# Gate and up of two chunks at a time with seven block products instead of eight, in three feed-forward stages

## The reference, cut to what matters

```python
h = (jax.nn.silu(u @ gate) * (u @ up)) @ down      # gate, up: 1024 x 2816, down: 2816 x 1024
```

## Time and profile before

| | us |
|---|---|
| median of 3 runs | 1923.45 (1923.35 to 1923.48) |
| the profiled execution | 1923.51 |
| its span | 1921.70 |
| busy in it: TensorE / weight loads | 1906.2 / 1682.8 |
| VectorE / ScalarE / GpSimd | 714.2 / 1083.8 / 1546.7 |

### The profile page before, as it was taken

One profiled execution on the slowest core, in us unless ns is written; L12 is line 12 of the kernel. 1 busy time (PEld: TensorE's weight loads), 2 busy tenths in 40 slices (PEclk: granted clock), 3 DMA queues, 4 the chain that ended last, 5 costly groups with the idle time before them and its releaser, 6 DMA issues.

```text
span 1921.7 us, 28382 instructions
## 1 busy us (share of the span) xinstructions
PE 1906.2 (99%) x11290; PEld 1682.8 (88%) x11290; DVE 714.2 (37%) x1440; ACT 1083.8 (56%) x1450; POOL 1546.7 (80%) x1228
## 2 busy tenths in 40 slices
PE   9999999999999999999999999999999999999998
PEld 7888999988888888889999888888999998888887
DVE  3222867521311222138574231113677632122112
ACT  7554674456644575456734665446666667545443
POOL 7998786666899799979776759997767787888995
PEclk9999999999999999999999999999999999999999
DMA  8554543143655565555323536555444444455552
GB/s 323 197 188 173 211 143 130 53 175 124 222 195 194 182 231 197 189 183 196 134 88 110 192 116 215 182 195 208 152 158 142 150 158 153 176 178 205 197 182 104
DMA packets 48803, 331.50 MB, mean 173 GB/s; under 512 B 5536, under 2 KB 6432, under 8 KB 10656
## 3 DMA queue, kind: packets, MB, share of 16 engines
q1 hardware_dynamic: 44208, 314.61, 45.6%
q10 hardware_dynamic: 4464, 15.09, 2.3%
HBM read 328.63 MB, written 1.05 MB: 172 GB/s over the span
## 4 chain that ended last, share of the span: by engine, by line
PE 96%; ACT 1%; DVE 1%; DMA 0%; issue 0%; ACTq 0%; DVEq 0%; SPq 0%
PE bank L2001 20%; PE bank L1967 16%; PE bank L1968 16%; PE bank L1969 16%; PE bank L2007 11%; PE bank L2115 2%; PE bank L2139 2%; PE bank L2117 1%; PE bank L2457 1%; PE bank L2473 1%; PE bank L2080 1%; ACT arena L431 1%; PE bank L2719 1%; PE bank L2579 1%; PE bank L2558 1%; PE bank L2129 0%
## 5 line engine op out<-in xcount | busy, mean ns | idle before, releaser
L400 POOL TENSOR_TENSOR wlo<-raw,whi 128x512 fp32r<-128x512 f32 x1180 | 1496.1, 1306 | 317.6 <-ACT whi L431 317.2
L431 ACT ACTIVATE whi<-raw 128x2048 fp32r<-128x2048 f32 (+1 forms) x298 | 566.8, 1904 | 189.2 <-PE bank L1969 161.8
L431 ACT ACTIVATE arena<-bank 128x512 f32<-128x512 f32 (+4 forms) x389 | 210.6, 551 | 441.4 <-PE bank L2007 265.3
L2001 PE MATMUL bank<-uT,whi 128*128 128x512 f32 x1632 | 388.9, 390 | 0.0
L2001 PEld LDWEIGHTS bank<-uT,whi 128*128 128x128 f32 x1632 | 302.8, 188 | 60.6
L1967 PE MATMUL bank<-uT,whi 128*128 128x256 f32 x768 | 222.5, 290 | 0.0
L1968 PE MATMUL bank<-uT,whi 128*128 128x256 f32 x768 | 217.1, 283 | 0.0
L1969 PE MATMUL bank<-uT,wlo 128*128 128x256 f32 x768 | 217.1, 283 | 0.0
L2007 PEld LDWEIGHTS bank<-uT,wlo 128*128 128x128 f32 x1632 | 209.2, 191 | 7.9
L2007 PE MATMUL bank<-uT,wlo 128*128 128x256 f32 x1632 | 211.7, 283 | 0.0
L1967 PE MATMUL bank<-whi,uT 128*128 128x512 f32 (+1 forms) x416 | 160.8, 387 | 0.0
(11 more groups left out here) (322 smaller groups left out, 2704.9 us busy)
## 6 DMA issues: line engine op xcount, KB each, us to landing
raw<-in_w SPq DMA_DIRECT2D x295, 1024.0 KB, 4.8
rows<-in_rows ACTq DMA_DIRECT2D x22, 512.0 KB, 5.0
raw<-in_w SPq DMA_DIRECT2D x4, 512.0 KB, 6.8
arena<-in_mem ACTq DMA_DIRECT2D x2, 1024.0 KB, 8.8
x<-in_x SPq DMA_DIRECT2D x2, 512.0 KB, 5.5
arena<-in_amask ACTq DMA_DIRECT2D x1, 576.0 KB, 6.3
out<-x SPq DMA_DIRECT2D x1, 512.0 KB, 2.7
out<-arena SPq DMA_DIRECT2D x1, 512.0 KB, 2.7
```

Source lines behind the costliest of these rows:

```text
L400: r = pool.tensor_tensor(wlo[n % LAND][:, k], raw[n % LAND][:, k], whi[n % RING][:, k].bitcast(F32), ALU.subtract)
L431: return act.activation(o, i, f, **k)
L2001: pe.matmul(both, w[0][:, c], parts[:, :, k, :], start=start and k == 0, stop=False)
```

## The change

For blocks i = 0 to 3 of each of the three stages, chunks c = 2 + 2i and c + 1 are taken together. With tokens in two halves, the 1024 inputs in two halves and the two chunks as column halves (each 256 gate and 256 up columns), the eight block products of 128 tokens x 512 inputs x 512 columns become seven: three on weights as they come (w11, w22, w21) and four on sums of weights (1: w12 - w11; 2: w22 - sum 1; 3: w22 - w12; 4: w21 - sum 2), with four sums of quarters of u. VectorE makes the sums in float32 and their low parts; ScalarE splits the four sums besides the units, so its list of splits (`ORDER`) has nine entries for two chunks; unit w12 is neither split by ScalarE nor by GpSimd. w21 lands in a slot of its own in the arena. All chunks are now computed by token, with four transposes for each. The partial sums of bank 4 are copied out by ScalarE between products and added by VectorE. The down units change their order (1, then 3 and 2, 5 and 4, 7 and 6, and at the end 9, 8, 10). The other two feed-forward stages are as before; semaphores `gate_sum`, `h_sum`, `up_low` and so on are merged. Waits on `unit_done` count places in the new order.

```diff
+BLOCKS = 4
+BLOCK_FFNS = [L * LAYER_UNITS + 69 for L in range(DEPTH)] + [DEPTH * LAYER_UNITS + 60]
+EXTRA = LAND
...
+def block_units(f, i):
+    n = BLOCK_FFNS[f] + 5 + (6 * i - 1 if i else 0)
+    return {"w11": n, "w12": n + 1, "w22": n + 2, "next_rows": n + 3, "w21": n + 4, "rows": n + 5 if i else None}
+def tensor_order():
+    order, n = [], 0
+    while n < N_UNITS:
+        if n - 5 not in BLOCK_FFNS:
+            order.append(n)
+            n += 1
+            continue
+        f = BLOCK_FFNS.index(n - 5)
+        for i in range(BLOCKS):
+            u = block_units(f, i)
+            order += [u["w11"], u["next_rows"], (f, i, 2), u["w22"], (f, i, 1), u["w21"], (f, i, 3)]
+            order += [u["rows"], (f, i, 4)] if i else [(f, i, 4)]
+        n = u["rows"] + 1
+    return order
+ORDER = tensor_order()
...
+PLACE = {o: q for q, o in enumerate(ORDER)}
+FULL = {block_units(f, i)["w12"]: (f, i) for f in range(len(BLOCK_FFNS)) for i in range(BLOCKS)}
+APART = [block_units(f, i)["w21"] for f in range(len(BLOCK_FFNS)) for i in range(BLOCKS)]
...
-                if n >= LAND:
-                    sp.wait_ge(sems["unit_done"], n - LAND + 1)
-                sp.dma_start(raw[n % LAND][:], a["w"][n]).then_inc(sems[f"raw_landed{n % LAND}"], 16)
+                before = [m for m in range(n) if SLOT[m] == SLOT[n]]
+                if before and before[-1] in FULL:
+                    sp.wait_ge(sems["sums_ready"], sums(*FULL[before[-1]], 3))
+                elif before:
+                    sp.wait_ge(sems["unit_done"], PLACE[before[-1]] + 1)
+                sp.dma_start(raw[SLOT[n]][:], a["w"][n]).then_inc(sems[f"raw_landed{SLOT[n]}"], 16)
...
+                pool.wait_ge(sems["w_hi"], q + 1)
+                if n in sums_read:
+                    pool.wait_ge(sems["sums_ready"], sums_read[n])
...
+                    n = ORDER[q]
+                    if n in SLOT:
+                        full = raw[SLOT[n]]
+                        act.wait_ge(sems[f"raw_landed{SLOT[n]}"], landed(n))
+                    else:
+                        full = wsum[n[2] - 1]
+                        act.wait_ge(sems["sums_ready"], sums(*n))
+                    if q >= RING:
+                        act.wait_ge(sems["unit_done"], q - RING + 1)
+                    fn(whi[q % RING][:], full[:], AF.Copy).then_inc(sems["w_hi"], 1)
...
+            def ffn_blocks(u0):
+                f = BLOCK_FFNS.index(u0)
+                chunk_by_token(u0, 0, lambda: activation_sums(f))
+                chunk_by_rows(u0, 1, False, True)
+                for i in range(BLOCKS):
+                    c = 2 + 2 * i
+                    u = block_units(f, i)
+                    if i:
+                        token_gate(c - 2, 1, 6)
+                    split()
+                    copy_part(0, 4, u["w11"])
+                    if i:
+                        token_hi(c - 2, 6)
+                    split()
+                    split()
+                    copy_part(1, 4, (f, i, 2))
+                    split()
+                    if i:
+                        split()
+                    copy_part(2, 4, (f, i, 1))
+                    token_gate(c + 1, 0, 7)
+                    split()
+                    split()
+                    token_gate(c, 0, 5)
+                    split()
+                    token_gate(c + 1, 1, 4)
+                    split()
+                    token_hi(c + 1, 7)
...
+            def copy_part(s, b, operand):
+                act.wait_ge(sems["unit_done"], PLACE[operand] + 1)
+                fn(part_copy[s], bank[b][:, :], AF.Copy).then_inc(sems["part_out"], 1)
...
+            def weight_sum(f, i, j, parts=(0, 1, 2, 3)):
+                u = block_units(f, i)
+                first, second = {1: ("w12", "w11"), 2: ("w22", 1), 3: ("w22", "w12"), 4: ("w21", 2)}[j]
+                for name in (first, second):
+                    if parts[0] == 0 and name in u:
+                        dve.wait_ge(sems[f"raw_landed{SLOT[u[name]]}"], landed(u[name]))
+                full = raw[SLOT[u[first]]]
+                less = raw[SLOT[u[second]]] if second in u else wsum[second - 1]
+                for n in parts:
+                    k = slice(n * quarter, (n + 1) * quarter)
+                    r = tt(wsum[j - 1][:, k], full[:, k], less[:, k], ALU.subtract)
+                if parts[-1] == 3:
+                    r.then_inc(sems["sums_ready"], 1)
+            def weight_sum_lo(f, i, j):
+                q = PLACE[(f, i, j)]
+                dve.wait_ge(sems["w_hi"], q + 1)
+                for n in range(4):
+                    k = slice(n * quarter, (n + 1) * quarter)
+                    r = tt(wsum_lo[j - 1][:, k], wsum[j - 1][:, k], whi[q % RING][:, k].bitcast(F32), ALU.subtract)
+                r.then_inc(sems["sum_lo"], 1)
+            def activation_sums():
+                dve.drain()
+                tt(u_full, uT[0].bitcast(F32), uT[1].bitcast(F32), ALU.add)
+                dve.drain()
+                u11, u12 = u_full[:, 0:4, 0:P], u_full[:, 4:8, 0:P]
+                u21, u22 = u_full[:, 0:4, P:SEQ], u_full[:, 4:8, P:SEQ]
+                tt(u_sums[:, 0], u21, u22, ALU.add)
+                tt(u_sums[:, 2], u11, u21, ALU.subtract)
+                dve.drain()
+                tt(u_sums[:, 1], u_sums[:, 0], u11, ALU.subtract)
+                dve.drain()
+                tt(u_sums[:, 3], u12, u_sums[:, 1], ALU.subtract).then_inc(sems["sums_ready"], 1)
+            def activation_sums_lo():
+                dve.wait_ge(sems["hi_part"], p.count("hi_part"))
+                tt(S_parts[1], u_sums.rearrange("p a b c -> p (a b c)"), S_parts[0].bitcast(F32), ALU.subtract)
...
+            def ffn_blocks(f):
+                activation_sums()
+                chunk_by_token(0)
+                weight_sum(f, 0, 1)
+                activation_sums_lo()
+                chunk_by_rows(1, False, None)
+                weight_sum(f, 0, 2)
+                weight_sum(f, 0, 3)
+                dve.drain()
+                weight_sum(f, 0, 4)
+                for i in range(BLOCKS):
+                    c = 2 + 2 * i
+                    more = i + 1 < BLOCKS
+                    weight_sum_lo(f, i, 2)
+                    if i:
+                        token_lo(c - 2, 6)
+                    weight_sum_lo(f, i, 1)
+                    weight_sum_lo(f, i, 3)
+                    dve.wait_ge(sems["part_out"], 3 * (f * BLOCKS + i) + 3)
+                    tt(bank[7][:, :], bank[7][:, :], part_copy[2], ALU.add).then_inc(sems["sum_out"], 1)
+                    if more:
+                        weight_sum(f, i + 1, 1)
+                    token_product(c + 1, 0, 7)
+                    dve.wait_ge(sems["unit_done"], PLACE[block_units(f, i)["w21"]] + 1)
+                    tt(bank[5][:, :], bank[5][:, :], part_copy[0], ALU.add).then_inc(sems["sum_out"], 1)
+                    weight_sum_lo(f, i, 4)
+                    token_product(c, 0, 5)
+                    dve.wait_ge(sems["unit_done"], PLACE[(f, i, 3)] + 1)
+                    tt(bank[4][:, :], bank[6][:, :], part_copy[2], ALU.add).then_inc(sems["sum_out"], 1)
+                    if more:
+                        weight_sum(f, i + 1, 2, (0, 1))
+                    token_product(c + 1, 1, 4)
+                    if more:
+                        weight_sum(f, i + 1, 2, (2, 3))
+                        weight_sum(f, i + 1, 3)
+                    token_lo(c + 1, 7)
+                    dve.wait_ge(sems["unit_done"], PLACE[(f, i, 4)] + 1)
+                    tt(bank[6][:, :], bank[6][:, :], part_copy[1], ALU.add).then_inc(sems["sum_out"], 1)
+                    if more:
+                        dve.drain()
+                        weight_sum(f, i + 1, 4, (0, 1))
+                    token_product(c, 1, 6)
+                    if more:
+                        weight_sum(f, i + 1, 4, (2, 3))
+                token_lo(CH - 3, 6)
+                chunk_by_token(CH - 1)
...
+                def block_product(operand, b, u, start, stop):
+                    q = PLACE[operand]
+                    hi = whi[q % RING]
+                    lo = wlo[SLOT[operand]] if operand in SLOT else wsum_lo[operand[2] - 1]
+                    pe.wait_ge(sems["w_hi"], q + 1)
+                    for k in range(4):
+                        pe.matmul(bank[b][:, :], u[0][:, k, :], hi[:, k * 512:(k + 1) * 512], start=start and k == 0, stop=False,
+                                  skip_group_check=not start)
+                    if operand not in SLOT:
+                        pe.wait_ge(sems["sum_lo"], p.count("sum_lo"))
+                    for k in range(4):
+                        pe.matmul(bank[b][:, :], u[1][:, k, :], hi[:, k * 512:(k + 1) * 512], start=False, stop=False,
+                                  skip_group_check=not start)
+                    if operand in SLOT:
+                        pe.wait_ge(sems["w_lo"], p.count("w_lo"))
+                    for k in range(4):
```

(48 more changed lines are left out.)

240 lines of the change are left out of this document (171 added, 69 removed).

## The result

The changed kernel takes 2088.78 us, median of four runs (2087.68 to 2089.49); the kernel before takes 1923.43 beside it. The ratio is 1.0859, 95% interval 1.084 to 1.0878: slower, by 165.3 us. The prediction was 2080.

What follows compares the result with a forecast made beforehand. TensorE bounds the kernel before; after the change VectorE and GpSimd, taking turns at the shared port, were to bind. 1923.5 us plus 53 for each of three stages gave 2082, rounded to 2080; range 1990 to 2140.

Steps and rivals of the forecast that it cites:

- TensorE's part: Per pair of chunks, four units go and seven products and transposes come: 31.0 us, gaining 2.1, or 25 to 26 overall.
- ScalarE's 21.8 us: ScalarE's splits, copies, high parts and half Silus in a pair: 21.8 us of 31, fitting beside TensorE.
- VectorE's part: Per pair, 32 two-SBUF-input instructions plus PSUM work cost 25.1 us alone, but take turns with GpSimd at 1.744 us.
- The tensor-scalar of the earlier trace: L1394, one input, SBUF to SBUF, cited among VectorE instructions lasting 1.34 to 1.63 us while GpSimd works.
- ports: Sum of port time, 1.254 us per GpSimd quarter plus 0.49 per VectorE instruction: 40.8 us a full pair, 185.3 a stage.
- queue: Sum of VectorE's queue, PSUM work, turns at 1.744 and the rest at 0.60: 42.6 us a full pair, 192.7 a stage.
- walk: Step-by-step walk through the engines' waits: 45.7 us a full pair, 210.4 a stage, each wait rounded up.
- the choice of the middle: Taking the middle between queue and walk, since one omits semaphore waits and the other rounds up: 53 us a stage.
- the tail keeps its length: The end of each changed stage, behind the last pair, was to stay at 27.8 us.
- Rival 1: The ports don't bind and TensorE stays the bound: 1923.5 - 26, plus 1.9 uncovered per stage, 1903 us; chance 0.07.
- Rival 2: TensorE's clock falls in its waits, 1.3 to 4.6 us a pair, 16 to 55 overall: 2096 to 2135 us; chance 0.20.
- Rival 3: The port is held for the whole instruction, 1.94 us a turn, 0.2 more each: 2122 us; chance 0.05.

Runs made afterwards that it cites:

- experiment 2: Changed kernel with the weight sums behind each stage's first pair and all sums' low parts replaced by one-input reductions of the same size; 1963.05 us.
- experiment 4: Changed kernel with GpSimd's subtractions for 28 units of each changed stage replaced by memsets, VectorE's instructions kept; 1945.70 us.
- experiment 1: Separate measuring kernel, none of the reference computed: 24 VectorE and 16 GpSimd subtractions of 128x512, apart and together; together medians 1735 and 1704 ns, alone 687 and 1262.
- experiment 7: Changed kernel with twelve zero-weight matmuls before TensorE's wait for the token products, ahead of each pair's second transposes; 2095.94 us.
- experiment 6: Changed kernel with VectorE also making the low parts of w11, w21, w22 and both down units, no GpSimd instruction in a pair; 2031.75 us.

## Why the prediction was right, and where it was off

**TensorE's part** held. A product at full clock takes 2.72 us in the changed kernel (1938.56 to 1941.28), predicted 2.73; a pair where nothing stops TensorE takes 30.9, predicted 31.0 (experiments 2 and 4). ScalarE's 21.8 us were 20.7, and hid.

**VectorE's part** held in its mechanism: the two engines take turns. Alone the pair costs VectorE 24.6 us, predicted 25.1; a turn is 1.70, taken as 1.744; for these instructions it is the reads that count (experiments 1, 2, 4). The tensor-scalar of the earlier trace rows, which has one input and took 1.34 us there, is a form that no run isolates. Here are three entries of the changed kernel: eight low parts while GpSimd works, four sums while it doesn't, and the first of the activation sums.

```profile
1937.09 13.47 DVE L1453 TENSOR_TENSOR wsum_lo<-wsum,whi 128x512 fp32r<-128x512 f32 x8
1951.07 2.48 DVE L1443 TENSOR_TENSOR wsum<-raw,raw 128x512 f32<-128x512 f32 x4
1848.27 3.22 DVE L1459 TENSOR_TENSOR arena<-uT 128x2048 f32<-128x2048 f32 x1
```

Eight in 13.47 are 1.68 each, four in 2.48 are 0.60 from start to start and the last 0.68. The activation sum of 128x2048, which I had taken as four of 512, took 3.22 us, less than half of the 7.0 that four turns would be. The sums' own lines came out at 0.76 to 1.32 us, where the forecast had 1.2 to 1.75 for all new lines.

**The stage**, term by term, in us:

| stretch | ports | queue | walk | measured, third stage |
|---|---|---|---|---|
| opening and first pair | 68.8 | 72.1 | 83 | 78.0 |
| second pair | 40.8 | 42.6 | 45.7 | 44.7 |
| third pair | 40.8 | 42.6 | 45.7 | 44.1 |
| last pair | 34.9 | 35.4 | 36 | 35.4 |
| tail | +0 | +0 | +0 | +2.8 |

Each stretch of this stage up to the tail lies between the queue sum and the walk, as the choice of the middle supposed: 202.2 us against 201.5 (148.5 + 53). That it came so near is partly luck. I had reasoned that the queue sum leaves out the waits. In the second pair VectorE hardly waits (0.1 us); it is busy for 44.6 instead of 42.6, because nearly all 20 quarters of GpSimd took turns and not 15.3. In the opening it is the other way round: VectorE is busy for 63.4, not 72.1, and waits 14.6. The last pairs of the other two stages took 34.1 and 33.9 us, below all three sums.

The sum before rounding was 1923.5 + 159 = 2082.5; the 6 us that it lacks are 3.4 in the third stage and 1.2 and 1.8 in the others. The step that failed in the third is "the tail keeps its length". From chunk 10 to the first addition to x it took 18.51 us and takes 21.35; of the 2.8, two waits of TensorE for GpSimd's low parts are 1.95 (0.43 at 2064.82, 1.52 at 2069.77; the other two stages have the second too, 1.50 and 1.51). GpSimd's timeline has the reason:

```profile
2044.12 25.50 POOL L485 TENSOR_TENSOR wlo<-raw,whi 128x512 fp32r<-128x512 f32 x20 [5.26 <-ACT whi L516]
```

It makes the last 20 quarters without a pause, 1.27 us each, and ends at 2069.62; it starts them late, since ScalarE's split for the first of them stands behind a half Silu that waits for VectorE's addition into bank 7 (2039.33), and that addition behind eight low parts in turns. The kernel before had its last quarter at 1900.43, 5.8 us ahead of the same point. In experiment 4 TensorE waits there too, for 1.58 us, but GpSimd pauses on the way (1.44 and 0.21 us) for splits that stand in ScalarE's queue behind work that waits for TensorE. This is read from the traces; no run tests it.

**The walk's details** were right in length rather than place. The opening went as described: activation sums for 10.0 us (predicted 10.5), TensorE waiting 2.85 for the first transposes (3.4), then 7.4 within product 2, for the low part of its sum, and 4.2 in three shorter waits ahead of it: 11.5 where I had some 14. In a full pair TensorE waits not once for 9.1 us but before both groups of transposes, 1.91 and 2.48 us in the second pair, 5.02 and 6.72 in the third, and some 1 to 1.5 us for low parts of sums.

**Rival 1** (the ports don't bind, 1903) fell: 125.7 us go when the contention is removed on VectorE's side (behind the first pair's sums), and 143.1 us on GpSimd's. Its price was wrong too. With the ports free in the stages the kernel takes 1945.7. I had given the opening 1.9 us of uncovered work; experiment 4 shows 60.1 where 49.2 less 2.1 and plus 1.9 would be 49.0. Those 11.1 and the tail's 2.0, three times, are 39 of the 43 us. So even with VectorE's instructions at 0.60 us the opening would have cost more (33 us) than the 25 to 26 us that TensorE gains.

**Rival 2** (the clock) was half right. The granted clock does fall, to 0.51 behind a wait of 5 us, which no row of before could show. Its price of 16 to 55 us on top of the forecast did not come: in the full pairs VectorE's queue covers it (experiment 7). The upper end was also added up wrongly: 3.2 - 1.9 + 2.7 is 4.0 us a pair and not 4.6, so 48 and not 55. What the clock costs in the opening stays open.

**Rival 3** (1.94 a turn) fell in its price by the 1.70 of experiment 1; what its mechanism has for it stands in the last section.

**A version that beats both** was not found. The best that still computes everything is experiment 6, 2031.75. To win, the sums' cost on VectorE would have to fall below TensorE's 30.9 a pair with GpSimd still splitting, and the opening would need its sums earlier. Neither was tried.

## What to carry to other kernels

Before work moves from a bound engine to an idle one, look at what the new instructions read, and price them in the presence of the engine that shares the port: VectorE at 37% and GpSimd at 80% had no room for 32 subtractions of 0.60 us a pair, because beside a subtraction of GpSimd's each takes 1.70. Then make three sums, by port, by queue and by a walk through the waits, and trust the queue sum least where the new instructions stand ahead of a short one that another engine waits for. If two engines take turns, try giving the work of both to the one that does it faster alone: low parts moved from GpSimd to the full VectorE made this kernel 42 to 57 us faster, though it stayed slower than the kernel before.

## What the runs showed of the hardware

The turns come close to a strict alternation where both engines have work: VectorE's 24 and GpSimd's 16 fit sixteen pairs of 1.70 us and eight of 0.60. What an instruction of VectorE adds to GpSimd's, 0.44 us, is less than the 0.60 it takes alone, so some of it must overlap. How long one waits for the other shows where a short instruction meets a long one, in the opening of the first changed stage:

```profile
513.30 2.28 DVE L1473 TENSOR_TENSOR memT<-arena,memT 128x2048 fp32r<-128x2048 f32 x1
513.52 3.21 POOL L485 TENSOR_TENSOR wlo<-raw,whi 128x512 fp32r<-128x512 f32 x1 [1.90 <-DVE wsum L1443]
```

GpSimd's quarter starts 0.22 us behind VectorE's instruction of 128x2048 and lasts until 1.15 us after that one's end, close to the whole 1.26 that it takes alone. So it did wait for the whole of VectorE's instruction, and a turn is shorter than the sum of both durations because their ends overlap. The long instruction takes 2.28 us when it starts first, as here, and the one at 1848.27, behind a quarter of GpSimd's, 3.22; four of 128x512 in turns would take 6.8, an estimate from the 1.70 of experiment 1.

And VectorE's queue can be faster with more work in it: 52 such instructions and none on GpSimd pass in 38.0 us, 32 beside GpSimd's 20 in 44.7.
